# First small loads begun by ACT beside SyncE's x, and A's biases multiplied ahead of the first projection

## The chip, the cores and the metric

The kernel runs on one core of a Trainium2 chip. The metric is the device time of one execution in microseconds. The kernel before takes 1155.94 us, the median of three timed runs between 1155.78 and 1157.33 us. The engines are named as in the profile: PE (TensorE, matrix multiplications), DVE (VectorE), ACT (ScalarE), POOL (GpSimd) and SP (SyncE, which begins transfers).

## The reference, cut to what matters

The program is an encoder trunk of two layers over 256 tokens of width 1024, in float32. What this case touches is the start of the first layer: the RMS norm of x, the combined input projection, and the learned bias of attention A, which looks at a 2-D neighbourhood of a token grid 64 wide.

```python
def mixer_sublayer(x, norm_g, w_in, qk_g, rpb, mix_g, w_out):
    h = rms_norm(x, norm_g)
    proj = h @ w_in                                   # 1024 x 2304
    qa, ka, va, qb, kb, vb, qc, kc, vc = jnp.split(proj, ...)
    ...
    oa = neighbourhood_attention(qa, ka, heads(va), rpb)   # 4 heads, scores + rpb[head, dr, dc]
    ob = dilated_attention(qb, kb, heads(vb))
    oc = gqa_attention(qc, kc, heads(vc))
    merged = jnp.concatenate([rms_norm(oa, ...), rms_norm(ob, ...), rms_norm(oc, ...)], axis=-1)
    return merged @ w_out

for l in range(DEPTH):                                # DEPTH = 2
    x = x + mixer_sublayer(x, ...)
    x = x + hier_moe(rms_norm(x, norm2_g[l]), ...)    # 32 experts, top 2 within the top group
```

## The kernel before

Each engine has its own program, written out in order by hand, and the programs meet at semaphores. `run_layers` (L351) calls `mixers(l)`, `first(l)` and then `item(l, i, q)` for eleven groups of experts, on every engine and for both layers. All loads are begun by SP, in the order of its program, and PE, DVE and ACT each take their own work strictly in order.

Weights come through a ring of 16 pieces and some regions beside it; `ring_plan` (L108) fixes which piece a load takes and which progress of PE frees it, and SP waits for that progress before it begins the load (L491 to L495 in `piece_in`, L511 to L517 in `whole_in`).

The mixers of the first layer begin as follows. SP (`mixers`, L530) begins ident (the unit matrix for turning), the first half of x (`x[:, 0]`, 128 tokens), the three rows of gains (`gain_loads`, L460), the first upper weights of group C (L560), the second half of x (`x[:, 1]`, L562), the lower weights and the second column part of C. For `g == 1` follow `bias_loads` (L464: the window rows of the learned bias, `na_rpb`, and `c_flip`, a unit matrix written backwards), `head_loads` (L468: the rope tables and the qk gains), `colmask` and the weights of group A.

PE (`mixers`, L938) runs two warm-up multiplications (`warm`, L743), turns the gains (`gains_turned`) and the first half of x (`half_turned(0, 0, j)`, banks 0 and 1), runs one more warm-up and starts `project(l, 0)`. A unit of the projection is one half of the tokens by one part of the columns, in eight steps of 128 rows of weights. Within unit 0, ahead of step 4, PE turns the second half of x (L774 to L777, banks 2 and 3). After units 0, 1 and 2 come A's biases (`biases`, L798, banks 0 to 3 in head order), then `turn_keys(l, 0)`, which waits for DVE's keys of group C, then unit 3 and on. Each call of `biases` multiplies the flipped unit matrix by overlapping window rows, and so lays out the learned bias of one head in a bank.

DVE (`mixers`, L1592) copies the gains, multiplies the turned x by the gains into hT (`rows_turned`, L1438, four operations in the order of the halves), takes units 0 and 1 out of the banks, reduces the keys' lengths, waits for POOL's roots and rope tables, makes the keys of C (`keys_c`, L1488), takes unit 2 out, makes the first queries, and then takes A's four biases out of the banks, each as a minimum with colmask (`biases`, L1458; `v_rel` counts them). ACT (`mixers`, L1313) squares the two halves of x for the norm (`x_squares`), and later the keys and queries. In the second layer the biases and gains are loaded and turned at the end of the first layer's experts, by other code.

Of the kernel before, what the change touches and what calls it, by code (L numbers as in the profile page):

```python
# [29 lines left out]
P = 128  # L30
# [3 lines left out]
KD = D // P  # L34
# [4 lines left out]
GRID = 64  # L39
# [124 lines left out]
def encoder(nc, a, out):  # L164
    ctx = ExitStack()
    with ctx:
# [9 lines left out]
        h = sb("h", [P, TT * D])  # L176
# [6 lines left out]
        colmask = sb("colmask", [P, GRID])  # L183
# [197 lines left out]

        LATE_BACK = 2

        def pair(i):
            return ((6, 7), (0, 1))[i % 2]

# [22 lines left out]
        def unit(i):  # L409

            g = GROUPS[i // 4]
            return g, i % 2, PARTS[g][i % 4 // 2]

        @block.sync
        def _(sp):
            extra = sp.alloc_register("sp_extra")
# [18 lines left out]
                sp.wait_ge(d_apart, 16 * APART_LOADS)  # L435
                sp.dma_start(hT_flat[:, 0:STAGED], apart).then_inc(d_rel, 16)

            def gain_source(l, n):
                name = ("norm1_g", "mix_norm_g", "norm2_g")[n]
                return a[name][l:l + 1].rearrange("l (k p) -> (l k) p", p=P)  # L440

            def window_rows(l, h0, n):

                first = a["na_rpb"][l:l + 1, 0:1, 4:11, 0:GRID // 2 - 1]
                return bass.AP(first.tensor, first.offset + 15 - (GRID - 1) + 465 * h0, [[1, GRID], [465, n], [1, 250]])

            APART_LOADS = 8

            def staged_apart():
# [6 lines left out]
                    sp.dma_start(apart[n * KD:(n + 1) * KD, P + 500:STAGED], gain_source(1, n)).then_inc(d_apart, 16)  # L456

                sp.dma_start(apart[3 * KD:P, P + 500:STAGED], a["c_ident"][3 * KD:P]).then_inc(d_apart, 16)

            def gain_loads(l):  # L460
                for n in range(3):
                    sp.dma_start(gain_rows[l][n * KD:(n + 1) * KD], gain_source(l, n)).then_inc(d_gains, 16)

            def bias_loads(l):  # L464
                sp.dma_start(staged[l][0:GRID, P:P + 1000].rearrange("p (h c) -> p h c", h=4), window_rows(l, 0, 4)).then_inc(d_rel, 16)
                sp.dma_start(staged[l][0:GRID, 0:P], a["c_flip"]).then_inc(d_rel, 16)

            def head_loads(l):  # L468
                if l:
# [59 lines left out]

            def mixers(l):  # L530
                if l == 0:
                    sp.dma_start(ident[:], a["c_ident"]).then_inc(d_ident, 16)
                    sp.dma_start(x[:, 0], xr[:, 0]).then_inc(d_x[0], 16)
                    gain_loads(l)
                for g in range(3):
                    if g == 1:
                        if l == 0:
                            bias_loads(l)
                        head_loads(l)
                        if l == 0:  # L540
                            sp.dma_start(colmask[:], a["c_colmask"]).then_inc(d_mask, 16)
                    if g == 2 and l == 0:
                        dil_load(l)
                        for name, dst in (("c_tri", tri), ("c_ones", ones)):
# [193 lines left out]
        def _(pe):  # L738
# [4 lines left out]
            def warm(b, n):  # L743

                for _ in range(n):
                    matmul(bank[b][:, 0:3 * P].rearrange("p (n s) -> p n s", n=3), ident[:],  # L746
                           ident[:].unsqueeze(1).broadcast_to([P, 3, P]), start=True, stop=True)
# [4 lines left out]
            def half_turned(l, t, j):  # L752

                if l == 0:
                    pe.wait_ge(d_x[t], 16)
                else:
                    pe.wait_ge(v_back[BACK.index((t, j))], l)
                for k in range(4):
                    last = transpose(bank[2 * t + j][:, k * P:k * P + P], x[:, t, (4 * j + k) * P:(4 * j + k + 1) * P], ident[:])
                last.then_inc(p_xT, 1)  # L760
# [177 lines left out]
            def mixers(l):  # L938
# [4 lines left out]
                    half_turned(l, 0, 0)  # L943
                half_turned(l, 0, 1)
                if l == 0:
                    warm(6, 1)
                project(l, 0)
                project(l, 1)
                project(l, 2)
                if l == 0:  # L950
                    for hd in range(4):
                        biases(0, hd, hd)
                turn_keys(l, 0)
                project(l, 3)
                turn_queries_c(l, 0)
# [255 lines left out]
        def _(act):  # L1211
# [94 lines left out]
            def rows_back(l):  # L1306
# [3 lines left out]
                for t in range(TT):  # L1310
                    copy(x[:, t].rearrange("p (c k) -> p k c", k=KD), x_kc[:, t]).then_inc(a_again, 1)

            def mixers(l):  # L1313
                if l == 0:
                    act.wait_ge(g_init, 4)
                x_squares(l, 0)
                x_squares(l, 1)
# [88 lines left out]
        def _(dve):  # L1406
# [28 lines left out]
                nc.vector.tensor_copy(gains[:], bank[b][:, 0:3 * KD]).then_inc(v_gains, 1)  # L1435
                dve.wait_ge(v_gains, l + 1)

            def rows_turned(l):  # L1438
                for t, j in ((0, 0), (0, 1), (1, 0), (1, 1)) if l == 0 else BACK:
                    dve.wait_ge(p_xT, 4 * l + (2 * t + j if l == 0 else 2 * j + t) + 1)  # L1440
                    tt(hT[:, 4 * j:4 * j + 4, t * P:t * P + P], bank[2 * t + j][:, :].rearrange("p (k s) -> p k s", k=4),  # L1441
                       wide(gains[:, 4 * j:4 * j + 4], P), ALU.mult).then_inc(v_xT, 1)
# [15 lines left out]
            def biases(l, hd, b):  # L1458
                if l == hd == 0:
                    dve.wait_ge(d_mask, 16)  # L1460
                dve.wait_ge(p_flip, 4 * l + hd + 1)
                tt(rel[:, hd], bank[b][:, 0:6 * GRID].rearrange("p (r c) -> p r c", c=GRID),
                   over(colmask[:], 1, 6), ALU.min).then_inc(v_rel, 1)
# [128 lines left out]
            def mixers(l):  # L1592
                if l == 0:
                    gains_turned(0, 7)
                rows_turned(l)
                projected(l, 0)
                projected(l, 1)
                head_lengths(l, "kC")
# [1 line left out]
                projected(l, 2)  # L1600
                head_lengths(l, "qC0", 0)
                queries_c(l, 0)
                if l == 0:
                    for hd in range(4):
                        biases(0, hd, hd)
                projected(l, 3)
                head_lengths(l, "qC1", 1)
                queries_c(l, 1)
# [351 lines left out]
```

## Time and profile before

| | |
|---|---|
| median of the timed runs | 1155.94 us (1155.78 to 1157.33, 3 runs) |
| span of the profiled execution | 1155.3 us |
| PE busy | 985.1 us, 85% |
| DVE, ACT, POOL busy | 291.5, 178.5, 51.6 us |
| loaded and stored | 437.07 MB, mean 378 GB/s |
| instructions | 13601 |

The span reaches from the first to the last instruction of one execution. A chain of work is followed back from the last instruction, at each step to what released it. Times within the span are counted from its start. The PE's program up to 12 us, SP's issues up to 13 us and the chain up to 82 us are the stretches that the change touches.

### The profile page before, as it was taken

How to read it: one execution, taken by the hardware profiler on the slowest of the kernel's cores; microseconds unless marked ns; L12 is line 12 of the kernel's file. 1: busy time of each engine (PE TensorE's matmuls, PEld its weight loads, DVE VectorE, ACT ScalarE, POOL GpSimd, SP SyncE). 2: the span in 40 equal slices, each digit the busy share in tenths (PEclk: the TensorE clock that was granted, in tenths of full speed). 3: DMA queues.
4: the chain of work that ended last, by engine and by line, in shares of the span. 5: the costliest groups of instructions: out<-in, count | busy, mean ns of one | idle time of the engine just before them, and what ended most of it. 6: DMA issues, size and time to landing. Idle time of an engine off the chain costs nothing.

```text
span 1155.3 us, 13601 instructions
## 1 busy us (share of the span) xinstructions
PE 985.1 (85%) x5408; PEld 462.8 (40%) x5408; DVE 291.5 (25%) x796; ACT 178.5 (15%) x444; POOL 51.6 (4%) x104
## 2 busy tenths in 40 slices
PE   8999999998887956548899999999969879474687
PEld 5556644353343412114355656444524334131242
DVE  3556552111110110001145565421111101100011
ACT  1244311110010100002024343111100001000110
POOL 2111100000000000000021211000000000000000
PEclk9999999999898987869999999999989889786799
DMA  9962889999999999999998248999999999999997
GB/s 315 332 271 110 349 308 417 425 426 427 428 428 427 427 428 428 427 427 421 401 395 316 105 175 335 356 420 427 430 427 428 426 429 428 427 428 428 427 418 286
DMA packets 61878, 437.07 MB, mean 378 GB/s; under 512 B 10909, under 2 KB 15349, under 8 KB 31349
## 3 DMA queue, kind: packets, MB, share of 16 engines
q1 hardware_dynamic: 61813, 436.17, 91.9%
q8 instruction: 45, 0.74, 0.3%
q14 instruction: 20, 0.16, 0.0%
HBM read 435.10 MB, written 1.44 MB: 378 GB/s over the span
## 4 chain that ended last, share of the span: by engine, by line
PE 62%; DMA 31%; DVE 2%; SPq 2%; issue 1%; POOL 1%; ACT 0%; DVEq 0%; POOLq 0%
PE bank L1078 31%; DMA ring<-in_w_down 16%; DMA ring<-in_w_gate 10%; PE bank L787 9%; DMA ring<-in_w_up 5%; PE bank L919 5%; PE bank L1104 5%; PE bank L1032 4%; PE bank L746 1%; PE bank L865 1%; PE bank L855 1%; SPq L528 1%; SPq L517 1%; PE bank L887 1%; DMA ring<-in_w_in 1%
## 5 line engine op out<-in xcount | busy, mean ns | idle before, releaser
L1078 PE MATMUL bank<-ring,work 128*32 128x512 f32 (+2 forms) x2608 | 482.5, 663 | 132.9 <-DMA ring<-in_w_up 51.6
L1078 PEld LDWEIGHTS bank<-ring,work 128*32 128x32 f32 (+2 forms) x2608 | 145.8, 130 | 396.1 <-issue 393.9
L787 PE MATMUL bank<-ring,hT 128*128 128x512 f32 (+1 forms) x384 | 128.3, 488 | 1.3 <-DVE hT L1441 0.8
L787 PEld LDWEIGHTS bank<-ring,hT 128*128 128x128 f32 x384 | 71.2, 190 | 48.8 <-issue 42.2
L1032 PEld LDWEIGHTS bank<-work,h 128*128 128x128 f32 x704 | 82.3, 192 | 16.5 <-issue 15.6
L1032 PE MATMUL bank<-work,h 128*128 128x128 f32 x704 | 86.8, 277 | 1.5 <-DVE work L1806 1.5
L1078 PE MATMUL bank<-work 128*32 128x512 f32 (+2 forms) x176 | 75.5, 620 | 12.0 <-DMA ring<-in_w_down 12.0
L1104 PE MATMUL bank<-work 128*128 128x512 f32 x176 | 81.4, 603 | 2.4 <-ACT work L1394 1.6
L1078 PE MATMUL bank<-kept,work 128*32 128x512 f32 (+1 forms) x160 | 74.3, 617 | 5.3 <-DMA ring<-in_w_up 5.3
L1862 DVE COPY work<-bank 128x512 f32<-128x512 f32 x20 | 13.8, 691 | 243.0 <-PE bank L1078 243.0
L1857 DVE TENSOR_TENSOR work<-work,bank 128x512 f32<-128x512 f32 x22 | 15.1, 688 | 220.0 <-PE bank L1078 220.0
L1828 DVE TENSOR_SCALAR work<-iota,work,rstd 128x128 f32<-128x128 f32 x80 | 22.3, 343 | 183.4 <-PE bank L1126 181.8
L919 PE MATMUL bank<-ring,h 128*128 128x512 f32 x128 | 58.2, 600 | 0.0
L1389 ACT COPY work<-bank 128x512 f32<-128x512 f32 x22 | 12.9, 586 | 274.1 <-PE bank L1151 274.1
L1385 ACT COPY work<-bank 128x256 f32<-128x256 f32 x22 | 8.2, 373 | 292.7 <-PE bank L1126 292.7
L1104 PEld LDWEIGHTS bank<-work 128*128 128x128 f32 x176 | 31.8, 189 | 50.9 <-issue 49.2
L1394 ACT COPY work<-bank 128x512 f32<-128x512 f32 x22 | 12.9, 586 | 172.3 <-PE bank L1078 155.9
L1078 PEld LDWEIGHTS bank<-work 128*32 128x32 f32 (+2 forms) x176 | 21.2, 135 | 38.0 <-issue 37.8
L746 PE MATMUL bank<-ident 128*128 128x384 f32 x88 | 33.8, 529 | 2.7 <-DMA ident<-in_c_ident 2.7
L919 PEld LDWEIGHTS bank<-ring,h 128*128 128x128 f32 x128 | 23.2, 190 | 25.3 <-issue 25.0
L1374 ACT ACTIVATE work<-bank,gain 128x128 f32<-128x128 f32 x88 | 25.2, 369 | 42.6 <-PE bank L1032 42.6
L666 POOL TENSOR_TENSOR ms<-ms,eps 128x1 f32<-128x1 f32 x20 | 3.8, 190 | 555.5 <-ACT h L1219 469.5
(212 smaller groups left out, 718.2 us busy)
## 6 DMA issues: line engine op xcount, KB each, us to landing
ring<-in_w_gate SPq DMA_DIRECT2D x42, 2048.0 KB, 24.9
ring<-in_w_down SPq DMA_DIRECT2D x38, 2048.0 KB, 23.8
ring<-in_w_up SPq DMA_DIRECT2D x36, 2048.0 KB, 29.4
ring<-in_w_up SPq DMA_DIRECT2D x36, 1024.0 KB, 14.7
ring<-in_w_down SPq DMA_DIRECT2D x28, 1024.0 KB, 10.9
ring<-in_w_gate SPq DMA_DIRECT2D x20, 1024.0 KB, 9.1
ring<-in_w_in SPq DMA_DIRECT2D x8, 1536.0 KB, 13.4
ring<-in_w_out SPq DMA_DIRECT2D x8, 1024.0 KB, 17.0
```

Of the source, the lines that this page charges most:

```text
L746: matmul(bank[b][:, 0:3 * P].rearrange("p (n s) -> p n s", n=3), ident[:], ident[:].unsqueeze(1).broadcast_to([P, 3, P]), start=True, stop ...
L787: last = matmul(bank[6 + i % 2][:, 0:c1 - c0], hT[:, k, t * P:t * P + P], group_in(l, gi)[:, k, c0:c1], start=(k == 0), stop=(k == KD - 1))
L919: last = matmul(bank[6 + n % 2][:, :], mixed[:, pos0 + c, t * P:t * P + P], rows(pos, 2)[:, c % 2, half * 512:half * 512 + 512], start=(c ...
L1032: last = nc.tensor.matmul(bank[banks[k // 4]][:, k % 4 * P:k % 4 * P + P], x_kc[:, t, k, :], pick[:, t, :], start=(t == 0), stop=(t == TT ...
L1078: last = nc.tensor.matmul(bank[b][e * w:e * w + w, :], lhs[:, k, e * w:e * w + w], rows(pos, k_count // 2)[:, kk, n * 512:n * 512 + 512], ...
L1104: last = nc.tensor.matmul(bank[SUM0 + n][:, :], pickT[:, t, :], y[:, half * 512:half * 512 + 512], start=(of == 0), stop=(of == NI - 1))
L1374: last = nc.scalar.mul(xg[:, k, :], bank[pair(i)[1]][:, (k - 4) * P:(k - 3) * P], gain2[:, q // NI, k:k + 1])
L1389: nc.scalar.copy(hidT.rearrange("p c s -> p (c s)"), bank[b0][:, :]).then_inc(a_hidT, 1)
L1394: nc.scalar.copy(y[:, 0:512], bank[b0][:, :]).then_inc(a_y, 1)
L1828: last = ts(hot[:, n], iota[:, 0:P], seats[:, TIME[i], n:n + 1], factors[n], ALU.is_equal, ALU.mult)
L1857: tt(hid, hid, bank[b1][:, :], ALU.mult).then_inc(v_hid, 1)
L1862: nc.vector.tensor_copy(y[:, 512:1024], bank[b1][:, :]).then_inc(v_y, 1)
```

## The change

SP no longer begins ident, the gains, the window rows, `c_flip` and colmask of the first layer. ACT does so, ahead of all its own work, in the order ident, three rows of gains, `c_flip`, window rows, colmask (`first_loads`). SP begins with the first half of x and goes on with the weights of C. PE multiplies A's biases ahead of unit 0, in banks 4, 5, 2 and 3 by head, in the place of the third warm-up multiplication; since the second half of x is turned into banks 2 and 3, PE now waits there until DVE has taken the biases of heads 2 and 3 out. DVE takes the biases out between the two halves of hT. `gain_source` and `window_rows` only move to where both programs can call them. The second layer is as it was.

```diff
--- before.py
+++ after.py
@@ -381,6 +381,8 @@
 
         LATE_BACK = 2
 
+        BIAS_BANKS = (4, 5, 2, 3)
+
         def pair(i):
             return ((6, 7), (0, 1))[i % 2]
 
@@ -411,6 +413,15 @@
             g = GROUPS[i // 4]
             return g, i % 2, PARTS[g][i % 4 // 2]
 
+        def gain_source(l, n):
+            name = ("norm1_g", "mix_norm_g", "norm2_g")[n]
+            return a[name][l:l + 1].rearrange("l (k p) -> (l k) p", p=P)
+
+        def window_rows(l, h0, n):
+
+            first = a["na_rpb"][l:l + 1, 0:1, 4:11, 0:GRID // 2 - 1]
+            return bass.AP(first.tensor, first.offset + 15 - (GRID - 1) + 465 * h0, [[1, GRID], [465, n], [1, 250]])
+
         @block.sync
         def _(sp):
             extra = sp.alloc_register("sp_extra")
@@ -434,15 +445,6 @@
                 kept_no_more(l - 1, TURNED_ROWS)
                 sp.wait_ge(d_apart, 16 * APART_LOADS)
                 sp.dma_start(hT_flat[:, 0:STAGED], apart).then_inc(d_rel, 16)
-
-            def gain_source(l, n):
-                name = ("norm1_g", "mix_norm_g", "norm2_g")[n]
-                return a[name][l:l + 1].rearrange("l (k p) -> (l k) p", p=P)
-
-            def window_rows(l, h0, n):
-
-                first = a["na_rpb"][l:l + 1, 0:1, 4:11, 0:GRID // 2 - 1]
-                return bass.AP(first.tensor, first.offset + 15 - (GRID - 1) + 465 * h0, [[1, GRID], [465, n], [1, 250]])
 
             APART_LOADS = 8
 
@@ -456,14 +458,6 @@
                     sp.dma_start(apart[n * KD:(n + 1) * KD, P + 500:STAGED], gain_source(1, n)).then_inc(d_apart, 16)
 
                 sp.dma_start(apart[3 * KD:P, P + 500:STAGED], a["c_ident"][3 * KD:P]).then_inc(d_apart, 16)
-
-            def gain_loads(l):
-                for n in range(3):
-                    sp.dma_start(gain_rows[l][n * KD:(n + 1) * KD], gain_source(l, n)).then_inc(d_gains, 16)
-
-            def bias_loads(l):
-                sp.dma_start(staged[l][0:GRID, P:P + 1000].rearrange("p (h c) -> p h c", h=4), window_rows(l, 0, 4)).then_inc(d_rel, 16)
-                sp.dma_start(staged[l][0:GRID, 0:P], a["c_flip"]).then_inc(d_rel, 16)
 
             def head_loads(l):
                 if l:
@@ -529,16 +523,10 @@
 
             def mixers(l):
                 if l == 0:
-                    sp.dma_start(ident[:], a["c_ident"]).then_inc(d_ident, 16)
                     sp.dma_start(x[:, 0], xr[:, 0]).then_inc(d_x[0], 16)
-                    gain_loads(l)
                 for g in range(3):
                     if g == 1:
-                        if l == 0:
-                            bias_loads(l)
                         head_loads(l)
-                        if l == 0:
-                            sp.dma_start(colmask[:], a["c_colmask"]).then_inc(d_mask, 16)
                     if g == 2 and l == 0:
                         dil_load(l)
                         for name, dst in (("c_tri", tri), ("c_ones", ones)):
@@ -753,6 +741,8 @@
 
                 if l == 0:
                     pe.wait_ge(d_x[t], 16)
+                    if t == 1:
+                        pe.wait_ge(v_rel, 3 + j)
                 else:
                     pe.wait_ge(v_back[BACK.index((t, j))], l)
                 for k in range(4):
@@ -943,13 +933,11 @@
                     half_turned(l, 0, 0)
                 half_turned(l, 0, 1)
                 if l == 0:
-                    warm(6, 1)
+                    for hd in range(4):
+                        biases(0, hd, BIAS_BANKS[hd])
                 project(l, 0)
                 project(l, 1)
                 project(l, 2)
-                if l == 0:
-                    for hd in range(4):
-                        biases(0, hd, hd)
                 turn_keys(l, 0)
                 project(l, 3)
                 turn_queries_c(l, 0)
@@ -1310,8 +1298,17 @@
                 for t in range(TT):
                     copy(x[:, t].rearrange("p (c k) -> p k c", k=KD), x_kc[:, t]).then_inc(a_again, 1)
 
+            def first_loads():
+                act.dma_start(ident[:], a["c_ident"]).then_inc(d_ident, 16)
+                for n in range(3):
+                    act.dma_start(gain_rows[0][n * KD:(n + 1) * KD], gain_source(0, n)).then_inc(d_gains, 16)
+                act.dma_start(staged[0][0:GRID, 0:P], a["c_flip"]).then_inc(d_rel, 16)
+                act.dma_start(staged[0][0:GRID, P:P + 1000].rearrange("p (h c) -> p h c", h=4), window_rows(0, 0, 4)).then_inc(d_rel, 16)
+                act.dma_start(colmask[:], a["c_colmask"]).then_inc(d_mask, 16)
+
             def mixers(l):
                 if l == 0:
+                    first_loads()
                     act.wait_ge(g_init, 4)
                 x_squares(l, 0)
                 x_squares(l, 1)
@@ -1435,8 +1432,8 @@
                 nc.vector.tensor_copy(gains[:], bank[b][:, 0:3 * KD]).then_inc(v_gains, 1)
                 dve.wait_ge(v_gains, l + 1)
 
-            def rows_turned(l):
-                for t, j in ((0, 0), (0, 1), (1, 0), (1, 1)) if l == 0 else BACK:
+            def rows_turned(l, parts):
+                for t, j in parts:
                     dve.wait_ge(p_xT, 4 * l + (2 * t + j if l == 0 else 2 * j + t) + 1)
                     tt(hT[:, 4 * j:4 * j + 4, t * P:t * P + P], bank[2 * t + j][:, :].rearrange("p (k s) -> p k s", k=4),
                        wide(gains[:, 4 * j:4 * j + 4], P), ALU.mult).then_inc(v_xT, 1)
@@ -1592,7 +1589,12 @@
             def mixers(l):
                 if l == 0:
                     gains_turned(0, 7)
-                rows_turned(l)
+                    rows_turned(0, ((0, 0), (0, 1)))
+                    for hd in range(4):
+                        biases(0, hd, BIAS_BANKS[hd])
+                    rows_turned(0, ((1, 0), (1, 1)))
+                else:
+                    rows_turned(l, BACK)
                 projected(l, 0)
                 projected(l, 1)
                 head_lengths(l, "kC")
@@ -1600,9 +1602,6 @@
                 projected(l, 2)
                 head_lengths(l, "qC0", 0)
                 queries_c(l, 0)
-                if l == 0:
-                    for hd in range(4):
-                        biases(0, hd, hd)
                 projected(l, 3)
                 head_lengths(l, "qC1", 1)
                 queries_c(l, 1)
```

## Rows read from the trace of the kernel before

**Rows 1.** The page: span and instructions; the chain's shares by engine.
```profile
span 1155.3 us, 13601 instructions
...
PE 62%; DMA 31%; DVE 2%; SPq 2%; issue 1%; POOL 1%; ACT 0%; DVEq 0%; POOLq 0%
```

**Rows 2.** Chain of work in order of time, to 82 us: start us, us, what.
```profile
3.77 7.94 DMA ring<-in_w_in
...
11.84 12.29 PE bank L787 x40
24.13 2.73 PE bank L806 x16
26.86 0.59 PE bank L821 x4
...
80.92 1.04 PE bank L878 x8
```

**Rows 3.** Timeline of PE, 2.5 to 12 us: start us, us, operation [idle before].
```profile
2.72 2.90 PE L746 MATMUL bank<-ident 128*128 128x384 f32 x4 [2.72 <-DMA ident<-in_c_ident]
...
5.78 1.38 PE L759 MATMUL bank<-ident,x 128*128 128x128 f32 x8
7.00 0.81 PE L746 MATMUL bank<-ident 128*128 128x384 f32 x2
7.69 1.97 PE L787 MATMUL bank<-ring,hT 128*128 128x256 f32 x8
10.29 1.09 PE L759 MATMUL bank<-ident,x 128*128 128x128 f32 x8 [0.63 <-DMA x<-in_x]
```

**Rows 4.** Busy time by stretch: us, five engines, then granted clock, DMA share, GB/s.
```profile
4.00:5.00 1.00, 1.00 (x3) 0.34 (x1) 0.00 (x0) 0.00 (x0) 0.00 (x0) 1.00 0.75 164
80.00:100.00 20.00, 19.08 (x114) 13.38 (x113) 14.19 (x33) 9.96 (x32) 7.00 (x12) 1.00 0.29 106
300.00:500.00 200.00, 146.46 (x838) 59.64 (x834) 21.31 (x53) 14.21 (x35) 0.00 (x0) 0.88 1.01 427
```

**Rows 5.** Waits of SP's queue: us in total, times, longest us.
```profile
SPq L495 <- PE bank L787: 40.7, 2, 29.7
```

**Rows 6.** Timeline of SP's issues, 0 to 13 us.
```profile
0.77 0.40 SPq L532 DMA_DIRECT2D ident<-in_c_ident  x1
1.23 0.42 SPq L533 DMA_DIRECT2D x<-in_x  x1
...
2.77 0.41 SPq L560 DMA_DIRECT2D ring<-in_w_in  x1
...
7.56 0.71 SPq L466 DMA_DIRECT2D work<-in_c_flip  x1
8.30 2.83 SPq L473 DMA_DIRECT2D kept<-in_c_rope  x2
```

**Rows 7.** Single transfers of the first 8 us: KB, us from issue to landing.
```profile
ident<-in_c_ident SPq DMA_DIRECT2D x1, 64.0 KB, 1.8
x<-in_x SPq DMA_DIRECT2D x1, 512.0 KB, 3.9
ring<-in_w_in SPq DMA_DIRECT2D x1, 512.0 KB, 4.8
work<-in_na_rpb SPq DMA_DIRECT2D x1, 250.0 KB, 11.3
```

**Rows 8.** Timeline of POOL and DVE, 17 to 26 us: towards the keys of C.
```profile
19.00 1.02 POOL L669 TENSOR_TENSOR rsh<-msh,mhalf 128x4 f32<-128x4 f32 x1
...
21.00 0.45 POOL L694 TENSOR_TENSOR kept<-kept 128x128 f32<-128x128 f32 x1 [0.98 <-DMA kept<-in_qk_norm_g]
...
24.65 0.76 DVE L1500 TENSOR_TENSOR work<-work 128x256 f32<-128x256 f32 x2
```

**Rows 9.** Lines 746 and 1462, to 45 us: duration ns min/median/max, first and last start.
```profile
L746 PE MATMUL bank<-ident x6: 486/847/978, 2.7 to 7.3; 128*128 128x384 f32 x6
...
L1462 DVE TENSOR_TENSOR kept<-bank,colmask x4: 545/547/551, 29.6 to 30.9; 128x384 f32<-128x384 f32 x4
```

## The prediction

> **What bounds the kernel now.** The first view to read is the page's span and its chain of work [rows 1]. The profiled execution spans 1155.3 us, against a median of 1155.94 us of the three timed runs (1155.78 to 1157.33), so about 0.6 us lies around the span; I carry differences over to the median one for one. PE holds 62% of the chain and the DMA of weights 31%. The change touches only the first 30 us, so the second view is the chain in order of time [rows 2]. Up to 11.84 us it consists of SP's issues and of the loads of the input projection. From 11.84 us on it is PE without a hole: 12.29 us of L787 (the rest of projection unit 0, then units 1 and 2), 2.73 us of L806 (A's biases), the turning of the keys L821 at 26.86 us, and so on to 80.92 us. A microsecond taken out of this stretch is therefore a microsecond, as long as nothing else comes late.
>
> The third view is PE's order up to 12 us [rows 3]. The warm-up multiplications run from 2.72 us, the first half of x is turned from 5.78 to 7.16 us, four of the eight steps of unit 0 run from 7.69 to 9.66 us, then PE waits for the second half of x (10.29 us) and again for the lower half of the weights (11.84 us). So PE does next to nothing in the 0.63 us before 10.29 and the 0.46 us before 11.84, and what it does in between can be pushed back a little only.
>
> Whether a shift in the first layer lasts to the end is seen in the weight stream. From 80 to 100 us the DMA engines are busy only 0.29 [rows 4], because SP stands before waits on PE, 29.7 us the longest of them on L787 [rows 5]. When the stream is full again later (1.01, 427 GB/s from 300 to 500 us [rows 4]), it started from a moment that PE's progress set. So a gain at the keys goes through the stream to the end, and I price it one for one.
>
> **The change, part by part.** (1) SP loses seven small issues ahead of or between the big ones. The first big weight load moves from 2.77 us to about 1.23 us [rows 6]: ident (0.46 us with the gap behind it) and the three gains (1.08 us, up to 2.77 us) are gone, 1.54 us in all. x moves from 1.23 to 0.77 us. From 4 to 5 us the DMA engines moved only 164 GB/s at a busy share of 0.75, against 427 GB/s of a full stream [rows 4]; so part of the early start is real. But ident, the gains and 314 KB of bias loads (250 KB window rows, 32 KB c_flip, 32 KB colmask) are now moved ahead of or among x and the weights. At 427 GB/s the 314 KB are 0.7 us. I take the second half of x and the lower weights about 0.8 us earlier than now (1.54 less 0.7), and the bounds are 1.54 us earlier and 0.7 us later. On the later part of SP's queue the rope and qk_norm loads move up by the issues taken out too; they are never the last in what follows.
>
> (2) PE's 2.73 us of biases [rows 2] leave the stretch behind 24.13 us and stand between the turning of the first half of x and unit 0. The single warm-up multiplication that goes with L946 ran from 7.00 us, while DVE was still at hT for the group that starts at 7.69 us [rows 3], so its removal is worth nothing.
>
> When can the biases begin? PE is free when the first half of x is turned, 7.16 us today. ident now lands in the company of x, which ACT and SP issue at the same time. Alone it took 1.8 us from its issue, and x took 3.9 us [rows 7]; if ident came only with x, it would be 2.1 us late. As it is an eighth of x's bytes I take 0.5 us late, so the warm-up ends later and PE is free at 7.66 us. The second condition is the landing of the window rows. By SP's issue times [rows 6] ACT needs 0.46 us for ident, 1.08 for the gains and 0.74 for c_flip (7.56 to 8.30 us), so that the window rows are issued at about 0.77 + 2.28 = 3.05 us. No row of before shows a load issued by ACT. The lowest bound for it is ident's 1.8 us (landing at 4.85 us, before PE needs it), the highest the 11.3 us that the same load took behind the weights on SP's queue (14.35 us) [rows 7]. The nearest row is the first 512 KB weight load, which landed 4.8 us after its issue with 576 KB of ident and x ahead of it; ahead of the window rows in their own queue are ident, the gains and c_flip, some 100 KB, and beside them is SP's queue. I take 4.8 us: landing at 7.85 us. The biases then run from 7.85 to 10.58 us, the first four steps of unit 0 take 1.97 us to 12.55, the second half of x is turned in 1.09 us to 13.64 [rows 3], and the second half of unit 0 starts at 13.64 us instead of 11.84: **1.80 us later**. The x and the lower weights have landed by then even at the late bound (10.29 + 0.7 and 11.71 + 0.7 us).
>
> The Trainium skill bears on this load. In "DMA: Bandwidth & Descriptors", section "Issuing engines are not separate DMA queues", it says that loads begun by several engines run on the same 16 DMA engines and interleave, and that only issue time is saved; the section "Queues, rings and completion order" says that each DMA engine takes turns between the queues. By the first the change could bring no more bandwidth than there is; by the second the window rows would not stand behind the whole of SP's queue, which is the 7.85 us rather than the 14.35 us. No row of before has a second issuing queue to show it.
>
> (3) The keys. Today L821 starts 1.45 us after DVE has finished the keys (24.65 + 0.76 = 25.41 us) [rows 8], since the biases stand between. With the biases gone this cover goes too. DVE's keys hang on unit 1 through ACT, DVE and POOL; POOL finished the root at 20.02 us and then stood 0.98 us for the qk_norm load, till 21.00 [rows 8]. With that load 1 us earlier, or the root later by 1.80 us, this wait closes, and the keys come at 25.41 - 0.98 + 1.80 = 26.23 us. PE ends unit 2 at 24.13 + 1.80 = 25.93 and waits 0.3 us for the keys. L821 starts at about 26.3 us instead of 26.86. **Sum: 2.73 out, 1.80 back, 0.3 to 0.4 for the keys: 0.5 us gained.**
>
> (4) DVE's four bias operations move from behind the queries to between the two halves of hT. They wait for colmask and PE's biases, and behind them stand the last two hT operations, for which units 0 and 1 wait. They take 0.55 us each [rows 9], and run while PE does the first half of unit 0; PE's new wait for v_rel before the second half of x is met if colmask is in by about 10 us. At nothing, then; if colmask came 1 us after that, PE would lose that 1 us. In their old place nothing is won: the chain has no wait on DVE from 27 to 80.92 us [rows 2]. ACT's own squares of x come some tenths later behind seven issues; the root they feed is needed only at unit 0's end. At nothing.
>
> The predicted time is 1155.94 - 0.5 = **1155.4 us**.
>
> **The rivals.** (a) *The full cover*: the window rows land before 7.16 us and ident is not late. Then the second half of unit 0 starts at 7.16 + 2.73 + 1.97 + 1.09 = 12.95 us, 1.11 us later, and the keys allow a gain of 26.86 - (24.43 + 1.11 + 0.05) = 1.3 us: 1154.6 us. Were the keys not late, it would be 1.6 us: 1154.3. The lower bounds of the loads speak for it, their company against it.
>
> (b) *Slower: PE stands before the biases for the window rows.* What speaks for it is the 11.3 us of that load, and that PE takes its work in order, so all of the first projection is queued behind this wait. Each microsecond beyond 7.85 us costs one. From a landing at 8.4 us nothing is won, and from 10.7 us on it is slower by more than 2.3 us. At 11.3 us, where the load would land if it came just behind the lower weights (11.71 less 0.8, plus 0.4 for its own length), the second half starts at 17.1 us, and the time is 1155.4 + 3.45 = 1158.9 us. Against it speaks that only some 100 KB stand ahead of it in ACT's queue.
>
> (c) *The biases run at the low rate.* The same warm-up multiplication takes 847 ns at first and 486 ns after the turning of x [rows 9], though the granted clock reads 1.00 from 4 to 5 us [rows 4], which is the 2.4 GHz level. If PE begins later, or stands idle before the biases, they might run at the slow pace: 2.73 x 847/486 = 4.76 us, 2.0 us more, and 1157.4 us. Against it: PE also stood idle twice between 9.66 and 11.84 us, and the 40 steps behind ran at full pace.
>
> (d) *More than the biases' place*: the early start also moves unit 0's second half ahead of 11.84 us. Then 2.7 us or more, 1153.2 us or less. For this PE would have to be done with the biases within its idle 1.1 us; the sum of (a) excludes that, unless the first weights and x come so early that the warm-up work falls away, and it is written out.
>
> **How the numbers follow.** A measurement of this kernel can tell about 0.2% from no change, 2.3 us. Chances: forecast 0.52, (a) 0.18, (b) 0.13 (nearly all of it slower by more than 2.3 us), (c) 0.12 (nearly all within), (d) 0.05. Faster 0.05, same 0.81, slower 0.14. The range goes from the end of (a) with 0.2 us of scatter, 1154.1 us, through (c), to the cheap half of (b), 1158.2 us.
>
> **What would show it.** In the profile after: L806 between the two halves of L759, starting near 7.9 us, with the wait ahead of it put down to the window rows; L787's long run starting near 13.6 us; L821 near 26.3 us, with its wait on DVE's keys; the same groups from there on, all 0.5 us earlier. A start of L806 after 10 us, or one L806 group longer than 4 us, would make the forecast wrong towards slower; L787's long run before 12 us would make it wrong towards faster.

## The result, and the profile after

The changed kernel takes 1164.05 us (median of 5 runs, 1162.34 to 1164.33) against 1155.94 us: ratio 1.0068, 95% interval 1.0058 to 1.0079. It is **8 us slower**, where 0.5 us faster was forecast with an upper bound of 1158.2 us. The profiled execution is the fastest of the five (1162.34 us, span 1160.5 us).

The page of the changed kernel, span and the new queue of ACT:

```profile
span 1160.5 us, 13599 instructions
...
q10 hardware_dynamic: 688, 0.40, 0.1%
```

The chain of work of the changed kernel in order of time (start us, us, what), to be laid beside [rows 2]:

```profile
3.15 8.98 DMA work<-in_na_rpb
12.17 4.66 PE bank L796 x16
16.83 3.39 PE bank L777 x8
20.23 0.87 PE bank L749 x8
21.10 5.20 PE bank L777 x24
...
33.47 0.66 PE bank L811 x4
...
87.60 1.04 PE bank L868 x8
```

Before, the chain went through the weights of the projection until 11.84 us. Now it goes through the load of the window rows until 12.13 us, then through the biases (L796), which take 4.66 us and not 2.73, and the first steps of unit 0 (L777), 3.39 us and not 1.97. The second half of unit 0 starts at 21.10 us instead of 11.84, the keys are turned (L811) at 33.47 instead of 26.86, and L868 at 87.60 us instead of 80.92 us has kept all of it: 6.7 us.

PE's timeline in the changed kernel, against [rows 3]:

```profile
5.40 2.90 PE L734 MATMUL bank<-ident 128*128 128x384 f32 x4 [5.40 <-DMA ident<-in_c_ident]
...
8.45 1.60 PE L749 MATMUL bank<-ident,x 128*128 128x128 f32 x8
12.17 4.66 PE L796 MATMUL bank<-work 64*64 64x384 f32 x16 [2.12 <-DMA work<-in_na_rpb]
```

PE starts 2.7 us late, because it waits for ident, and then stands 2.12 us before the biases. The transfers of the changed kernel (KB, us from issue to landing), against [rows 7]:

```profile
x<-in_x SPq DMA_DIRECT2D x1, 512.0 KB, 4.3
ident<-in_c_ident ACTq DMA_DIRECT2D x1, 64.0 KB, 4.5
work<-in_c_flip ACTq DMA_DIRECT2D x1, 32.0 KB, 6.0
work<-in_na_rpb ACTq DMA_DIRECT2D x1, 250.0 KB, 9.0
```

ident, alone on the engines before, landed after 1.8 us; begun at the same moment as x, it lands with x. c_flip, with 32 KB, took 6.0 us, so it is not the window rows alone that come late in ACT's queue. The third part is the clock, in the busy time by stretch (the third number from the end of a row is the granted clock):

```profile
11.00:12.00 1.00, 0.00 (x0) 0.00 (x0) 0.00 (x0) 0.00 (x0) 0.00 (x0) 1.00 1.04 252
13.00:14.00 1.00, 1.00 (x6) 0.26 (x4) 0.56 (x1) 0.00 (x0) 0.00 (x0) 0.50 1.04 381
18.00:19.00 1.00, 1.00 (x3) 0.79 (x3) 0.00 (x0) 0.00 (x0) 0.00 (x0) 0.50 1.03 399
20.00:21.00 1.00, 1.00 (x11) 0.93 (x9) 0.30 (x1) 0.00 (x0) 0.00 (x0) 1.00 1.03 402
```

After the two idle microseconds before 12.17 us PE works at 0.50 of its clock, the 1.2 GHz level, for most of the biases and of unit 0's first steps.

### The profile page after: what moved, and what is told of

The parts are those of the page before. It is cut to its first block, busy times and chain, and to the rows that moved or that the text cites. A ratio compares the mean times of both kernels' runs of the same rounds, so it can differ in the third digit from the quotient of the medians.

```text
span 1160.5 us, 13599 instructions
## 1 busy us (share of the span) xinstructions
PE 985.7 (85%) x5406; PEld 463.2 (40%) x5406; DVE 291.9 (25%) x796; ACT 178.1 (15%) x444; POOL 51.6 (4%) x104
## 4 chain that ended last, share of the span: by engine, by line
PE 62%; DMA 32%; DVE 3%; POOL 1%; SPq 1%; issue 1%; ACTq 0%; ACT 0%; DVEq 0%; POOLq 0%
PE bank L1066 31%; DMA ring<-in_w_down 16%; DMA ring<-in_w_gate 10%; PE bank L777 9%; DMA ring<-in_w_up 5%; PE bank L1092 5%; PE bank L909 5%; PE bank L1020 4%; PE bank L855 1%; PE bank L734 1%; PE bank L845 1%; DMA work<-in_na_rpb 1%; SPq L511 1%; PE bank L877 1%; PE bank L1084 1%
## 5 line engine op out<-in xcount | busy, mean ns | idle before, releaser
L777 PE MATMUL bank<-ring,hT 128*128 128x512 f32 (+1 forms) x384 | 129.8, 492 | 0.8 <-DVE hT L1438 0.8
L777 PEld LDWEIGHTS bank<-ring,hT 128*128 128x128 f32 x384 | 72.3, 193 | 49.2 <-issue 43.3
L1020 PEld LDWEIGHTS bank<-work,h 128*128 128x128 f32 x704 | 82.3, 192 | 16.5 <-issue 15.6
L1020 PE MATMUL bank<-work,h 128*128 128x128 f32 x704 | 86.8, 277 | 1.6 <-DVE work L1805 1.6
## 6 DMA issues: line engine op xcount, KB each, us to landing
ring<-in_w_up SPq DMA_DIRECT2D x36, 1024.0 KB, 14.3
ring<-in_w_in SPq DMA_DIRECT2D x8, 1536.0 KB, 14.3
```

The lines of the kernel that those rows point to most:

```text
L777: last = matmul(bank[6 + i % 2][:, 0:c1 - c0], hT[:, k, t * P:t * P + P], group_in(l, gi)[:, k, c0:c1], start=(k == 0), stop=(k == KD - 1))
L1020: last = nc.tensor.matmul(bank[banks[k // 4]][:, k % 4 * P:k % 4 * P + P], x_kc[:, t, k, :], pick[:, t, :], start=(t == 0), stop=(t == TT ...
```

## The experiments

The theory after this reading: PE is late because ident and then the window rows land late, and the idle time brings the low clock. The rivals: the late ident alone carries the loss; the new order of PE and DVE costs in itself, whatever the loads do; the idle time and the clock are not connected. Kernels measured together ran on one chip and share the runs of the kernel before; between sections ratios are compared, not times.

### Ident begun by SP again

```diff
+                    sp.dma_start(ident[:], a["c_ident"]).then_inc(d_ident, 16)   # SP, ahead of x
-                act.dma_start(ident[:], a["c_ident"]).then_inc(d_ident, 16)
```

> The changed kernel with one edit: SP begins the unit matrix (ident) ahead of x, as before the change; ACT begins the other six loads. Theory (the window rows bind): the unit matrix lands near 2.6 us instead of 5.4, PE's warm-up and the turning of x end near 7.2 us instead of 10.05, but the window rows still land near 11.7 us (begun 0.45 us earlier on ACT), so PE idles 4.5 us instead of 2.1, the biases again run slowly (4.7 us), and the keys are turned some 0.4 us earlier than in the changed kernel: about 1163.6 us against its 1164.05. Rival (the late unit matrix is the price): everything moves up by its 2.7 us, 1161.4 us.

Measured: 1162.36 us, ratio to before 1.0057 (1.0042 to 1.0071). PE's timeline and the load:

```profile
2.68 2.90 PE L735 MATMUL bank<-ident 128*128 128x384 f32 x4 [2.68 <-DMA ident<-in_c_ident]
...
5.73 1.97 PE L750 MATMUL bank<-ident,x 128*128 128x128 f32 x8
10.88 5.39 PE L797 MATMUL bank<-work 64*64 64x384 f32 x16 [3.18 <-DMA work<-in_na_rpb]
...
work<-in_na_rpb ACTq DMA_DIRECT2D x1, 250.0 KB, 8.2
```

PE starts 2.7 us earlier and is no better off: it stands 3.18 us before the biases. The rows land at 10.83 us, a little ahead of what was expected, but the biases then take 5.39 us, and the keys are turned at 34.20 us, later than the 33.47 of the changed kernel. The turning of x, with 1.97 us against 1.38 in [rows 3], shows that PE was still at the low pace when this wait began. The time lies between the 1163.6 us of the theory and the 1161.4 us of its rival, and its interval overlaps that of the changed kernel, so it is the timeline that decides. The late ident is not what the loss hangs on as long as the rows come later still.

### The loads alone

```diff
 # loads as in the change; PE and DVE as before
+                    warm(6, 1)
-                    for hd in range(4):
-                        biases(0, hd, BIAS_BANKS[hd])
                 project(l, 0)
                 project(l, 1)
                 project(l, 2)
+                if l == 0:
+                    for hd in range(4):
+                        biases(0, hd, hd)
```

> ACT begins the seven loads as in the changed kernel, but PE and DVE keep the order of before (third warm-up multiplication, biases behind unit 2, banks 0 to 3). Theory: PE starts at 5.4 us as in the changed kernel, the first half of x is turned by 10.05 us, four steps of unit 0 run to 12.7 us at the full pace, the second half of unit 0 starts near 13.8 us against 11.84 before; the keys are turned near 28.8 us (26.86 before), so about 2 us slower than before, 1157.9 us. Rival (the order of PE and DVE is the price and not the loads): no slower than before, about 1154.5 us with weights 1.5 us earlier.

Measured: 1157.48 us, ratio 1.0015 (1.0007 to 1.0024). Its chain:

```profile
0.79 4.38 DMA ident<-in_c_ident
...
28.43 0.59 PE bank L809 x4
```

The keys are turned at 28.43 us, 1.6 us later than in [rows 2], near the 2 us expected. So the seven loads on ACT cost 1.4 to 1.8 us by themselves, through ident, and most of the loss needs the new order as well.

### PE kept at work during the wait

```diff
                 if l == 0:
+                    warm(6, 3)
                     for hd in range(4):
                         biases(0, hd, BIAS_BANKS[hd])
```

> The changed kernel with three warm-up multiplications between the turning of x and the biases, so that PE works while the window rows are on their way. Theory (the clock fell because PE was idle): the granted clock stays at 1.00 up to 20 us, the biases take 2.75 us instead of 4.66 and the first half of unit 0 1.97 us instead of 3.4; the warm-up ends near 12.5 us, 0.3 us after the rows; the keys are turned about 2.9 us earlier, 1161.1 us against 1164.05. Rival (the biases run slowly for another reason, or the idle time does not matter): still 4.7 us, and 0.3 us slower, 1164.4 us.

Measured: 1158.74 us, ratio 1.0027 (1.0017 to 1.0038). PE's timeline:

```profile
9.47 2.10 PE L734 MATMUL bank<-ident 128*128 128x384 f32 x6
12.04 2.80 PE L796 MATMUL bank<-work 64*64 64x384 f32 x16 [0.46 <-DMA work<-in_na_rpb]
14.77 1.99 PE L777 MATMUL bank<-ring,hT 128*128 128x256 f32 x8
```

The rows land as late as ever, but the biases take 2.80 us and the first steps 1.99, and the keys are turned at 30.00 us, 3.5 us before those of the changed kernel. Three multiplications whose result nobody reads take back 5 of the 8 us, more than the 2.9 us expected. The two profiled spans lie 5.0 us apart (1160.5 and 1155.5), 1.5 us more than the keys; where that part comes from was not followed up. The rival without a connection of idle time and clock has fallen. The Trainium skill, "TensorE: Matmul & The Clock Gate", section "What's actually happening", says that the low clock is the default and activity releases it; this pair of runs agrees.

### The window rows from elsewhere, and in longer rows

In the changed kernel the 256 rows overlap in a table of 7.4 KB. The first edit reads as many rows of the same length from a stretch without overlap, the second reads as many bytes as 64 rows of 4000. Both leave out the true bias of the first layer. The edits are cut to the address of the rows.

```diff
+                rows = bass.AP(a["w_gate"]..., [[1024, GRID], [256, 4], [1, 250]])   # elsewhere
+                rows = bass.AP(a["w_gate"]..., [[1024, GRID], [1, 1000]])            # long rows
-                window_rows(0, 0, 4)
```

> The changed kernel, with the 250 KB of window rows read from a stretch of 256 KB in which no two rows overlap (a part of the gate weights) instead of from overlapping windows of a table of 7.4 KB per layer; number and length of the rows are the same. The learned bias of A in the first layer is thereby wrong, all work is the same. Theory (the load waits its turn beside SP's stream): it lands 9 us after its issue as in the changed kernel, 1164 us. Rival (many reads of the same few KB of memory are slow): it lands 6 us after its issue or sooner, PE's wait of 2.1 us goes, the clock stays up, 1158 to 1160 us.

> The changed kernel with the same 250 KB into the same place, but as 64 rows of 4000 bytes instead of 256 rows of 1000, read from the gate weights (the learned bias of A in the first layer is thereby wrong, all other work is the same). With the stream behind it held, the load still landed 8.0 us after its issue, so something in the load itself is slow. Theory (short rows are slow of themselves, and slow what runs beside them): it lands 6 us after its issue or sooner, ahead of 10 us, and the DMA rate does not drop to 250 GB/s from 8 to 12 us; PE's wait is gone or under 0.5 us. Rival (it is the place in ACT's queue behind four other loads, or the 64 lanes): 8 to 9 us after its issue, as before.

Measured: 1164.81 us, ratio 1.0079 (1.0062 to 1.0096), and 1163.71 us, ratio 1.0061 (1.0041 to 1.0081). The loads, one from each:

```profile
work<-in_w_gate ACTq DMA_DIRECT2D x1, 250.0 KB, 9.0
...
work<-in_w_gate ACTq DMA_DIRECT2D x1, 250.0 KB, 7.9
```

The overlap is not the reason: 9.0 us as before. The length of the rows is 1.1 us of it at most, 7.9 us, and in the long rows' run too the engines move only 192 GB/s from 8 to 9 us at a busy share of 0.98. The theory of the short rows, which expected 6 us or less, has fallen.

### The second weights held back

```diff
                                 ks = slice(half * 4, half * 4 + 4)
+                                if l == half == 0 and n == 1:
+                                    sp.wait_ge(d_rel, 32)
```

> The changed kernel, in which SP begins the second column part of C's weights (2 MB) and all that follows only when the window rows and c_flip have landed; up to there SP's stream is x and the first column part, 2 MB. Theory (the window rows share the engines with SP's stream, and the stream makes them late): they land near 9 us instead of 12.1, ahead of PE's end of turning x at 10.05 us, PE does not idle, the biases take 2.75 us, the second half of unit 0 starts near 15.7 us, the keys are turned near 28.3 us: 1157.6 us. Rival (the 256 short rows are slow of themselves): they land near 12 us again, and with the later weights it is at or above the 1164 us of the changed kernel.

Measured: 1162.39 us, ratio 1.0051 (1.0035 to 1.0066). The load, PE's timeline, and the stretches ahead of the landing:

```profile
work<-in_na_rpb ACTq DMA_DIRECT2D x1, 250.0 KB, 8.0
...
8.16 1.97 PE L751 MATMUL bank<-ident,x 128*128 128x128 f32 x8
11.11 5.38 PE L798 MATMUL bank<-work 64*64 64x384 f32 x16 [0.97 <-DMA work<-in_na_rpb]
...
9.00:10.00 1.00, 1.00 (x6) 0.73 (x4) 0.61 (x1) 0.00 (x0) 0.71 (x2) 1.00 0.93 177
10.00:11.00 1.00, 0.13 (x1) 0.00 (x0) 0.78 (x2) 0.00 (x0) 0.00 (x0) 1.00 0.09 11
```

The rows land at 11.06 us; neither the 9 us of the theory nor the 12 of its rival. The bytes are through by about 10 us (11 GB/s after that). So the 2 MB and the small loads held with them are worth 1.0 of the 9.0 us. PE stands only 0.97 us before the biases, and they still take 5.38 us: here, as with ident on SP, the turning of x had taken 1.97 us, so the clock was low before the wait began and could not fall in it (the clock's column reads 1.00 there all the same; see the last section). What x, the first weights and the place behind four other loads are worth beside it was not separated.

### The order alone

```diff
 # all loads on SP as before; PE and DVE as in the change
```

> All loads on SP in the order of before; PE and DVE in the order of the change. Theory (PE stands before the biases until the window rows and c_flip are there): c_flip lands near 19.7 us as before, PE idles from 7.2 us, the biases and the first half of unit 0 run at the low clock (4.7 and 3.4 us), the second half of unit 0 starts near 29.6 us instead of 11.84, the keys are turned 15 us later than before: 1171 us. Rival (the order is harmless): 1156 us.

Measured, in one run: 1172.61 us. PE's timeline, and the granted clock while it waits:

```profile
18.89 5.38 PE L810 MATMUL bank<-work 64*64 64x384 f32 x16 [11.29 <-DMA work<-in_c_flip]
...
8.00:9.00 1.00, 0.00 (x0) 0.00 (x0) 0.35 (x1) 0.00 (x0) 0.75 (x2) 1.00 0.96 294
12.00:13.00 1.00, 0.00 (x0) 0.00 (x0) 0.00 (x0) 0.00 (x0) 0.00 (x0) 0.50 1.05 408
```

PE stands 11.29 us for c_flip, the clock falls during the wait, and the keys are turned at 41.18 us, 14.3 us late. So moving the loads forward did help the new order, by 8 us as far as one run tells; it helped too little.

### Ident on SP, old order, and the gains alone on ACT

```diff
 # first: six loads on ACT, ident on SP, PE and DVE as before
 # second: the kernel before with only this moved
-                    gain_loads(l)
+                    for n in range(3):
+                        act.dma_start(gain_rows[0][n * KD:(n + 1) * KD], gain_source(0, n)).then_inc(d_gains, 16)
```

> SP begins the unit matrix ahead of x, ACT begins the other six loads, PE and DVE keep the order of before. Theory (beside the window rows only the late unit matrix cost something): PE starts at 2.7 us and turns the first half of x by 7.2 us; the lower weights land between 10.8 and 11.5 us, since SP begins them 1.1 us earlier and the window rows share the engines with them; the keys are turned 0.3 to 1.0 us earlier than the 26.86 us of before: 1155.1 to 1155.7 us, no measurable change. Rival (issuing loads from ACT costs in itself): near the kernel with all seven loads on ACT in the old order, 1157.5 us.

> The kernel before, with the three rows of gains alone begun by ACT. SP begins the first weights, the second half of x and the lower weights 1.1 us earlier, and nothing of size is moved ahead of them. Theory: the lower weights land near 10.7 us instead of 11.71, unit 0's second half and the keys move up by 0.9 to 1.0 us: 1155.0 us against 1156.0. Rival (the first transfers share the engines so that the early start gives nothing): 1156 us, the lower weights still landing near 11.7 us.

Measured: 1156.14 us, ratio 1.0005 (0.9996 to 1.0014), and 1155.27 us, ratio 1.0004 (0.9995 to 1.0013), against 1155.2 us of before on that chip. From the chain of the first, then of the second:

```profile
2.74 9.28 DMA ring<-in_w_in
12.16 12.29 PE bank L776 x40
...
10.69 12.05 PE bank L782 x40
...
25.47 0.58 PE bank L816 x4
```

With six loads on ACT the lower weights are begun 1.0 us earlier, take 9.3 us instead of 7.9, and unit 0's second half starts at 12.16 us instead of 11.84: the small loads beside them eat the whole head start. With only the gains moved the second half starts at 10.69 us and the keys are turned at 25.47 us, 1.1 to 1.4 us earlier, as the theory had it. Its time shows none of that: 0.9 us would be a ratio of 0.9992, below the interval. No kernel tried here beats the one before measurably.

### Ident on SP and PE kept at work

```diff
+                    sp.dma_start(ident[:], a["c_ident"]).then_inc(d_ident, 16)   # SP, ahead of x
-                act.dma_start(ident[:], a["c_ident"]).then_inc(d_ident, 16)
+                    warm(6, 4)                                                   # PE, ahead of the biases
```

> The changed kernel with the unit matrix begun by SP ahead of x, and four warm-up multiplications ahead of the biases, so that the clock is the same question in both cases. Theory (the window rows bind, and the late unit matrix only as it delays them): rows land near 10.9 us as in the run with the unit matrix on SP, the biases start near 11.2 us at the full pace, second half of unit 0 near 16.8 us, keys near 29.1 us: 1157.8 us, 0.9 us below the kernel with the warm-up alone. Rival (the late unit matrix costs its 2.7 us once the clock is held): keys at 27.3 us, 1156.0 us.

Measured: 1158.29 us, ratio 1.0015 (1.0005 to 1.0025). The load, begun at 2.68 us, and from the chain:

```profile
work<-in_na_rpb ACTq DMA_DIRECT2D x1, 250.0 KB, 7.9
...
7.95 2.84 PE bank L735 x8
10.78 2.73 PE bank L797 x16
...
28.68 0.66 PE bank L812 x4
```

The biases start at 10.78 us instead of 12.04 and run at the full pace; the keys are turned 1.3 us before those of the kernel with the warm-up alone, not 2.7. PE does not wait for the rows here, which landed near 10.6 us: the four multiplications (L735) hold it until 10.78 us. Fewer of them could have gained 0.2 us at most, so the early ident could not have given back its 2.7 us. Even with ident in time and the clock held, the new order is 1.7 us slower than before by the ratio.

### Both kernels again

> The kernel before, unchanged, as a second profile of it. Theory (the profile shown of before is one of its slower executions: the clock fell to 0.50 from 139 to 143 us, where all profiles since kept 1.00): the keys are turned at 26.9 us again, the first gathering of the experts starts at 144.3 us instead of 145.28, span 1153.5 to 1154.5. Rival (the keys themselves start at another time in most executions): keys beyond 26.5 to 27.3 us. Time: no difference, ratio 1.000 within 0.001.

> The changed kernel again, as a second profile and for its time on the same chip as the others. Theory (four of its five first executions took 1.5 to 2 us longer than the profiled one because the clock was low for longer in the first 25 us): the biases take up to 5.4 us and the second turning of x up to 1.9 us, the keys are turned between 33.5 and 34.5 us, span 1161 to 1162.5, 1163 to 1164.5 us. Rival (the rest is lost elsewhere): keys at 33.5 us and the span still near 1162, with a stage behind 30 us that is longer than in the first profile.

Measured on one chip: before 1155.42 us, ratio 0.9996 (0.9986 to 1.0006) to the other runs of the same kernel; changed 1163.68 us, ratio 1.0063 (1.0049 to 1.0077). From the chain of before, then PE's timeline of the changed kernel and a stretch of it:

```profile
11.56 12.28 PE bank L787 x40
...
26.58 0.59 PE bank L821 x4
...
12.14 5.38 PE L796 MATMUL bank<-work 64*64 64x384 f32 x16 [2.07 <-DMA work<-in_na_rpb]
17.45 3.62 PE L777 MATMUL bank<-ring,hT 128*128 128x256 f32 x8
...
13.00:14.00 1.00, 1.00 (x6) 0.29 (x4) 0.20 (x1) 0.00 (x0) 0.00 (x0) 1.00 1.06 389
```

The second profile of before has the keys at 26.58 us, the first gathering of the experts (L1032) at 143.99 us instead of 145.28, and a span of 1153.6 us, which is 1.8 us less than its time of 1155.39. In the profile shown ahead of the prediction the clock fell in the router stage, which it did not in the second:

```profile
140.00:142.00 2.00, 2.00 (x6) 1.39 (x7) 1.65 (x10) 1.67 (x1) 0.00 (x0) 0.50 0.99 414
...
140.00:142.00 2.00, 1.91 (x6) 0.76 (x5) 1.72 (x11) 1.37 (x1) 0.00 (x0) 1.00 1.03 426
```

The changed kernel's second profile is slower than its first: biases 5.38 us, keys at 34.31 us, span 1162.9 us. It too has the low clock in the router stage, and its first profile has not. From the chain of the second up to the first gathering (L1020 here), then the gathering in the first:

```profile
144.19 3.94 PE bank L924 x32
148.13 3.24 PE bank L734 x6
152.80 3.81 PE bank L1020 x32
...
150.94 3.81 PE bank L1020 x32
```

So like has to be laid beside like. In the two profiles without the low clock there, the second of before and the first after, the keys lie 6.9 us apart (26.58 and 33.47), the first gathering 6.95 us (143.99 and 150.94) and the spans 6.9 us: **the whole difference is there at the keys** and goes through. Between the two second profiles 7.7 us lie at the keys (26.58 and 34.31), 8.8 us at the first gathering and 9.3 us at the spans: 1.1 us of this came in between, where the router stage lies, and 0.5 us later. The medians of the same chip lie 7.6 to 8.3 us apart (1163.68 against 1156.13 and 1155.42). The low clock in the router stage is no rarity, other than the expectation says: six of the fourteen profiles show it, one of before and one of the changed kernel among them.

## Why the prediction was wrong

The loss is rival (b), which stood at 0.13 in the text, with rival (c) on top of it, which was priced as if it came alone. Both signs named there for a slower outcome came: the biases started after 10 us (12.17), and their group took more than 4 us (4.66). In order of the steps, predicted and read in the first profile after:

| step | predicted | measured |
|---|---|---|
| PE later for ident | 0.5 us | 2.68 us |
| window rows landed | 7.85 us | 12.13 us |
| biases on PE | 2.73 us | 4.66 us (5.38 in the second profile) |
| first steps of unit 0 | 1.97 us | 3.39 us (3.55) |
| second half of unit 0 starts | 13.64 us | 21.10 us (21.94) |
| wait for the keys behind unit 2 | 0.3 us | 0.3 us |
| keys turned | 26.3 us | 33.47 us (34.31) |

**ident** failed in the term that took about a quarter of the late bound. The bound of 2.1 us itself was right in kind (ident lands with x) and a little small; an eighth of the bytes was no reason for an earlier landing, since both are begun together. The Trainium skill, "DMA: Bandwidth & Descriptors", section "Issuing engines are not separate DMA queues", says that loads begun by different engines interleave on the same DMA engines; the rows agree, with 4.5 us for ident beside 4.3 us for x.

**The window rows** failed most. The 4.8 us of the first weights were taken as the nearest row, because little stands ahead of the rows in ACT's own queue. They took 9.0 us, nearer to the 11.3 us of SP's queue. The range given for the load, 1.8 to 11.3 us, held it; the value in it did not, and the range of the time was cut at a landing near 10.7 us. By the text's own price of one microsecond each, a landing at 12.13 us was 4.3 us more, 1159.7 us.

**The clock** failed as a sum. (c) was priced at 2.0 us for the biases alone and held against the forecast, not against (b). But (b) is idle time, and with it goes the low clock: the run with PE kept at work through the wait shows it. In the first profile after and in the order alone the clock fell in the wait; in the changed kernel's second profile, with ident on SP and with the second weights held, the turning of x shows that it had not yet risen. The low clock cost 1.9 to 2.7 us at the biases and 1.4 to 1.6 us at the first steps of unit 0 in the two profiles. The steps of unit 0, which stand right behind, were left out of the price. The argument against (c), that PE had stood idle twice before 11.84 us without harm, used waits of 0.63 and 0.46 us, behind work at the full pace, for one of 2.

**What held**: the cover of the keys is gone and costs the 0.3 us that were priced; the biases' four operations on DVE hide; a shift at the keys goes through. In single profiles the keys of the gains-alone kernel and of the loads-alone kernel lie 2.96 us apart (25.47 and 28.43), the first gathering 2.95 (142.88 and 145.83), the first item's long wait for w_down 2.91 (270.52 and 273.43); the spans lie 2.4 us apart and the ratios 1.3 us, so of so small a shift not all is seen in the time. The time around the span was wrong: 1.8 us, not 0.6, because the profiled execution was not the median one; this moved no term.

Two things stay open. Why the rows take 8 to 9 us was not settled: not overlap, little from the length of the rows, 1 us from the loads behind. A kernel with the rows at the head of a queue was not tried. And the gains-alone kernel, with its keys 1.1 us earlier than the second profile of before and its span 0.4 us shorter, shows no gain in time; its profile has 1.1 us still at 270 us and 0.8 us at the second layer's first turning (577.05 against 577.89), so something is given back later, or single profiles do not stand for the median.

## What to carry to other kernels

A load moved to a second queue can lose the head start that it had in the first one, as ident did (1.8 us before, 4.5 us after): a 64 KB load that PE's start hangs on belongs ahead of the big ones, in their queue. Before work is moved into a hole of an in-order engine, find the landing of its operands at the new place, and price a miss as the wait plus the low clock for the work behind it (here 3.4 to 4.2 us in the two profiles). Where such a wait can't be avoided, multiplications that nobody reads are cheap insurance: here three of them took back 5 us, 3.5 of them at the keys.

## What had not been expected of the hardware

Whether PE has reached the full clock by 10 us differs between executions of one program. In the first profile after, the turning of x took 1.60 us and the clock fell at 13 us; in the second it took 1.97 us, and the biases ran at the low pace from their first to their last, 5.38 us. In that profile the granted clock reads 1.00 all the while, as the row from 13 to 14 us above shows. At the start of these traces the durations tell the clock, and the column does not: 5.38 us are twice the 2.73 of before.

While the window rows are on their way, the engines move few bytes at a full busy share: 206 GB/s from 16 to 17 us in the second profile of before, at a busy share of 1.19, and 192 GB/s with long rows from 8 to 9 us. Other small loads were on their way beside them, so what makes the engines slow there, the 64 lanes or something else, was not separated.
